# Within-chunk output products of a chunked scan, computed by halves of the chunk's rows (64 stationary columns each)

## What is computed

```python
def step(state, inp):
    xdt_c, dA_c, B_c, C_c = inp
    acum = jnp.cumsum(dA_c, axis=1)
    seg = acum[:, :, None] - acum[:, None, :]
    decay = jnp.exp(jnp.where(causal, seg, -jnp.inf))
    cb = jnp.einsum('blgn,bsgn->blsg', C_c, B_c)
    y_diag = jnp.einsum('blsg,blsgr,bsgrp->blgrp', cb, decay, xdt_c)
    y_off = jnp.einsum('blgn,bgrpn,blgr->blgrp', C_c, state, jnp.exp(acum))
    ...
    return new_state, y_diag + y_off
```

## Time and profile before

| | |
|---|---|
| median of three runs | 1881.79 us (1881.12 to 1885.85) |
| span of the profiled execution | 1879.9 us |
| PE busy | 1780.4 us (95%) |
| PE weight loads busy | 1236.6 us (66%) |
| DVE busy | 913.8 us (49%) |
| ACT busy | 718.1 us (38%) |
| POOL busy | 695.7 us (37%) |
| mean granted TensorE clock | 0.976 |

### The profile page before, as it was taken

How to read it: one execution, slowest core, us unless ns; L and a number is a source line. 1 busy time by engine, 2 the same in 40 slices (tenths; PEclk the granted TensorE clock), 3 DMA queues, 4 the chain that set the end, 5 groups by cost and what they waited for, 6 DMA issues and landing times. The chain is left out here.

```text
span 1879.9 us, 29242 instructions
## 1 busy us (share of the span) xinstructions
PE 1780.4 (95%) x9708; PEld 1236.6 (66%) x9708; DVE 913.8 (49%) x2041; ACT 718.1 (38%) x1854; POOL 695.7 (37%) x799
## 2 busy tenths in 40 slices
PE   6999999999998899999999999999998999999994
PEld 3444444687454688888887546468546888888882
DVE  5687754687123454334334622057344634434347
ACT  0443200465023554544444401044235454444541
POOL 1333300165122685554543410300144955554540
PEclk9999999999999899999999999999998999999997
DMA  9865567731105799999996603100237999999964
GB/s 335 308 233 191 191 206 244 255 134 37 64 23 194 258 333 352 330 330 323 330 325 145 219 30 135 57 1 1 73 138 273 321 331 332 318 335 347 335 161 165
DMA packets 170255, 409.50 MB, mean 218 GB/s; under 512 B 37652, under 2 KB 45188, under 8 KB 170164
## 3 DMA queue, kind: packets, MB, share of 16 engines
q1 hardware_dynamic: 132724, 337.77, 50.0%
q0 software_dynamic: 37440, 70.56, 15.1%
HBM read 394.23 MB, written 79.75 MB: 252 GB/s over the span
## 5 line engine op out<-in xcount | busy, mean ns | idle before, releaser
L1336 ACT ACTIVATE arena<-psum,lncol 128x128 f32<-128x128 f32 x1024 | 371.5, 468 | 416.1 <-PE psum L834 416.1
L856 PE MATMUL psum<-arena 128*128 128x128 f32 x4096 | 501.1, 278 | 0.0
L856 PEld LDWEIGHTS psum<-arena 128*128 128x128 f32 x4096 | 478.4, 193 | 1.0 <-issue 1.0
L1871 DVE COPY arena<-arena 128x1 f32 (+1 forms) x128 | 19.7, 154 | 463.8 <-PE psum L856 321.6
L868 PE MATMUL psum<-arena 128*128 128x512 f32 x512 | 241.0, 593 | 0.7 <-DVE arena L1889 0.7
L2250 POOL DMA_INDIRECT expert_sum<-arena,idx x124 | 199.0, 1605 | 39.9 <-issue 38.7
L1889 DVE SCALAR_TENSOR_TENSOR arena<-psum,arena 128x512 f32<-128x512 f32 x256 | 182.0, 744 | 15.0 <-PE psum L868 14.8
L834 PEld LDWEIGHTS psum<-ident,arena 128*128 128x128 f32 x1024 | 122.0, 143 | 74.3 <-issue 64.3
L2221 POOL TENSOR_TENSOR passed<-ones 128x1 f32<-128x1 f32 x252 | 50.4, 200 | 302.3 <-DVE arena L1889 290.8
L2237 POOL DMA_INDIRECT arena<-h_rows,idx x128 | 139.7, 1091 | 19.2 <-issue 4.2
L616 PE MATMUL psum<-arena 128*128 128x512 f32 x320 | 145.5, 616 | 0.0
(11 more groups left out here) (285 smaller groups left out, 2320.6 us busy)
## 6 DMA issues: line engine op xcount, KB each, us to landing
arena<-in_moe_w_dram SPq DMA_DIRECT2D x384, 512.0 KB
arena<-in_ada_w_dram SPq DMA_DIRECT2D x38, 1024.0 KB, 5.2
arena<-in_ssm_w_in_dram SPq DMA_DIRECT2D x9, 2048.0 KB, 11.3
arena<-in_ada_w_dram SPq DMA_DIRECT2D x5, 2048.0 KB, 10.1
arena<-in_ssm_w_out_dram SPq DMA_DIRECT2D x4, 2048.0 KB, 9.1
expert_sum<-arena SPq DMA_DIRECT2D x4, 2048.0 KB, 15.5
arena<-expert_sum SPq DMA_DIRECT2D x16, 512.0 KB, 6.1
arena<-in_kv_ada_w_dram SPq DMA_DIRECT2D x4, 1024.0 KB, 5.9
```

The costliest lines, as they stand in the source:

```text
L856: mm = pe.matmul(psum[:, b, 0:P], w[:, k, :], xeT[u % 2][:, k, :], start=(k == 0), stop=(k == KC - 1))
L1336: ins = act.activation(xeT[u % 2][:, k, :], psum[:, b, P * j:P * j + P], ACT.Identity, scale=h_scale(l, k), bias=h_shift(l, k))
```

## The change

Each of the eight within-chunk products of a step becomes two. The first uses columns 0 to 63 of the head's `mixm` as stationary operand and writes partitions 0 to 63 of bank 7; the second uses columns 64 to 127 and writes partitions 64 to 127. The moving operand, 128 rows by 64 columns, is the same for both. All other instructions, waits and signals stay, and the last product of the step still signals bank 7. Apart from that the file loses blank lines, so that line numbers behind it are smaller by 21 (L689 becomes L670).

```diff
                 for h in range(GH):
                     if h % 4 == 0:
                         pe.wait_ge(mixm_ready, 2 * q + h // 4 + 1)
-                    mm = pe.matmul(ps[:, HD * h:HD * h + HD], mixm[h // 4][:, P * (h % 4):P * (h % 4) + P],
-                                   xdt[q % 2][:, HD * h:HD * h + HD], start=True, stop=True)
+                    for rows_ in (slice(0, HD), slice(HD, P)):
+                        of = slice(P * (h % 4) + rows_.start, P * (h % 4) + rows_.stop)
+                        mm = pe.matmul(ps[rows_, HD * h:HD * h + HD], mixm[h // 4][:, of],
+                                       xdt[q % 2][:, HD * h:HD * h + HD], start=True, stop=True)
                 fill(mm, 7, ("yd", q))
```

## The result

The changed kernel takes **1874.4 us** (median of five runs, 1873.19 to 1875.85) against 1881.79 us, 7.4 us less. The ratio of the runs is 0.9957, 95% interval 0.9944 to 0.9969 (the two medians alone give 0.9961). The mechanism is that of rival A; the forecast was wrong.

A forecast was written before the change was run, and what follows sets the result against it. The prediction took PE to bound the scan, with DVE close behind. Pairs (+0.09 us) and width change (+0.30 us) over 16 steps, less 0.3 us hidden, gave +6.0 us: 1887.8 us, range 1877 to 1907 us.

The forecast's parts named there:

- rival A: Within-chunk products: both array halves work side by side, 0.029 us a pair; -4 us because of DVE, 1878 us; chance 26%.
- What bounds the kernel: PE bounds the scan, DVE close behind; a shift of the scan's end reaches the program's end unchanged.
- (a): Load-and-matmul pairs of the within-chunk products: 32 at 0.057 us, halves taking turns, instead of 16; +0.09 us per step.
- (b): Switching to the narrower output and back around the within-chunk products: 0.15 us each way, +0.30 us per step.
- (c): Sum over the scan: 0.39 us x 16 steps = 6.3 us, less 0.3 us hidden in the last steps; +6.0 us.
- Rival B: Within-chunk products: loads can't run beside the other half's matmul, or each half change empties the array; 1899 to 1916 us; 22%.
- rival C: Around the within-chunk products: the change of width costs nothing, leaving +1.4 us, 1883 us; chance 7%.

The follow-up runs named there:

- e7: Kernel before the change, with DVE's copy of B moved to ACT for chunks 0 to 2 and left out in chunk 3: ratio 1.0006, scan 109.99 us.
- e11: Kernel before the change, with POOL's state scaling for the next step put between this step's add and gate: ratio 1.0003, scan 109.83 us.
- e14: Kernel before the change, with POOL's add and gate cut from 512 columns to one: ratio 0.9988, scan 106.98 us.
- e2: Changed kernel, but of each four heads first the four lower halves, then the four upper: 1881.83 us, ratio 0.9998 to the kernel before.
- e3: Changed kernel, but only the first head's product by halves, the seven others whole: 1886.09 us, ratio 1.0023 to the kernel before.
- e5: Changed kernel, but halves only in the seven steps where DVE showed no wait for the products: ratio 0.9995 to the kernel before, scan 107.03 us.
- e4: Changed kernel, but each head's product as four with 32 stationary columns: 1875.98 us, ratio 0.9966 to the kernel before, scan 102.96 us.
- e13: Changed kernel, with POOL's add and gate cut from 512 columns to one: ratio 0.9947 to the kernel before, scan 98.49 us.

## Why the prediction was wrong

- **What bounds the kernel** was right: PE bounded the scan (e7, e11 and e14 leave its steps as long as they were, but for the last one in e14), and the scan's gain reached the end.
- **(a), the pairs: the step that failed.** "I take 0.057 because L689, L516 and L596 all show a load running beside a matmul, and none shows two matmuls side by side." In turns a pair of 64 columns does cost 0.055 us (e2's first loads), but alternating halves don't take turns: 0.028 us. So the term was not +0.09 us per step but about -0.80. No row of before could show this, since none had two halves; the absence of a row was taken as evidence for turns. The bound on the other side, 0.029 us, was right to a nanosecond.
- **(b), the change of width**, +0.30 us per step, was right: e3 measures +0.22 per step of scan against +0.20 to +0.25 by these prices, and the step of the changed kernel is 1.08 us from L670 to L636, with 0.10 more ahead of L670, so 1.18 - 32 x 0.028 = 0.28 us for the two changes of width.
- **(c), the sum**, +6.0 us, falls with (a). By the measured prices a step is about 0.5 us shorter on PE (4.65 instead of 5.15 in chunk 0), 8 us in all, as under rival A.
- **Rival A** had the mechanism, with 26%, and the wrong size: "Nine steps could take their 0.50 us, the other seven about nothing". e5 shows that the seven give 2.8 us. PE's gain in one step is a lead that lasts to the next wait of DVE, so the cap was DVE's idle time summed over the stretch, 6.3 us of waits for L689 and some more, and not its waits one by one. That is why the time lay below the range's lower end, 1877.
- Rival B (a load that can't run beside the other half's matmul) and rival C (a free change of width) are out: by the 0.028 us and by e3. The Trainium skill's "TensorEngine Tiling (Array Packing)", Key Properties, has tiles load and multiply in parallel, and this case's trace agrees, at 0.028 us a pair instead of 0.055. The rule there that a change of mode drains the engine agrees too, with 0.10 us ahead of L670.

## What to carry to other kernels

Where a product is bound by its weight load (here 128 stationary columns, 64 moving ones, float32), alternating halves of the array about halve its time, at 0.3 us for going there and back. A whole product costs 0.22 us here, one by halves 0.11, so by this estimate three in a row pay for the way; a single one doesn't (e3). Alternate the halves: in groups of four most of the gain is lost (e2). When an engine gets faster, cap the gain by the next engine's idle time over the whole stretch, not step by step: here a lead lasted until the next wait. How far the buffers would let it grow wasn't tested. And look at what the next engine's busy time is made of; here over a third of L1592's 33.6 us went when POOL's instructions shrank.

## What was not expected of the hardware

- Four parts of 32 columns run at once, matmuls 0.014 us apart on average (e4), in plain float32 products.
- The engine starts the other half's pairs while the last three of its own group are still to be issued (e2, as read from the starts of the loads).
- DVE and POOL hold each other up where both work from SBUF. The pair of L1592 takes 1.28 us alone and 2.35 to 3.06 beside POOL; POOL's gate takes 1.27 us where DVE's pair doesn't run and 1.60 to 1.65 beside it. The Trainium skill's "SBUF — State Buffer", section "Who interferes with whom", describes a pair of ports shared by the two engines as an exclusive lock. This case's trace agrees: 13 us of DVE's time went when POOL's instructions shrank (e13), and of a pair beside the gate it is the second L1592 that is long, ending 0.56 us behind the gate.
